# A hybrid decoder trunk on one core: the second weight slab's first quarter is brought and used ahead of the first slab, and one query copy and one partial mean change engines

## What is computed

```python
def even_mixer(xn, pos, lb, w_in, hgrn_gain, w_out):
    h = jnp.einsum('bsd,de->bse', xn, w_in)
    aq, af, ai, bq, bk, bv, z = jnp.split(h, splits, axis=-1)
    oa = hgrn2_chunked(heads(aq), heads(af), heads(ai), lb)   # gated recurrence
    ...
# in hgrn2_chunked:
    f = lbb + (1.0 - lbb) * jax.nn.sigmoid(to_chunks(f_logit))
    k = 1.0 - f
    b = jnp.cumsum(jnp.log(f), axis=3)
    q_dec = qc * jnp.exp(b)
    k_inv = k * jnp.exp(-b)
```

## Time and profile before

| | |
|---|---|
| times of three runs | 586.45, 587.00, 587.67 us (median 587.0) |
| the profiled execution | 587.2 us, its span 585.5 us |
| mean granted TensorE clock | 0.998 of full speed |
| PE busy | 575.8 us (98% of the span) |
| DVE, ACT, POOL busy | 416.2, 384.9, 73.3 us |
| read from HBM | 96.16 MB, 166 GB/s over the span |
| chain that ended last | PE 96%, ACT 1%, DVE 1%, DMA 1% |

### The profile page before, as it was taken

One profiled execution on the slowest core, in us unless ns is written; L12 is line 12 of the kernel. 1 busy time (PEld: TensorE's weight loads), 2 busy tenths in 40 slices (PEclk: granted clock), 3 DMA queues, 4 the chain that ended last, 5 costly groups with the idle time before them and its releaser, 6 DMA issues.

```text
span 585.5 us, 9718 instructions
## 1 busy us (share of the span) xinstructions
PE 575.8 (98%) x3868; PEld 532.9 (91%) x3868; DVE 416.2 (71%) x645; ACT 384.9 (66%) x583; POOL 73.3 (13%) x77
## 2 busy tenths in 40 slices
PE   7999999999999999999999999999999999999995
PEld 6999989999999898889988999999899998888985
DVE  6878579446977684567666874799997974766663
ACT  6854685278397575657666846969758837556764
POOL 4230005001003910100000001102120200100002
PEclk9999999999999999999999999999999999999999
DMA  9756364446624964465444544336644463356201
GB/s 297 251 180 222 89 201 143 146 143 217 208 81 150 282 217 144 153 232 190 144 144 163 198 151 177 128 123 213 218 144 145 161 234 128 128 213 219 104 1 73
DMA packets 51856, 98.88 MB, mean 169 GB/s; under 512 B 1732, under 2 KB 7140, under 8 KB 51812
## 3 DMA queue, kind: packets, MB, share of 16 engines
q1 hardware_dynamic: 50628, 96.95, 49.2%
q0 software_dynamic: 1024, 1.05, 0.7%
q10 hardware_dynamic: 160, 0.27, 0.1%
HBM read 96.16 MB, written 1.05 MB: 166 GB/s over the span
## 4 chain that ended last, share of the span: by engine, by line
PE 96%; ACT 1%; DVE 1%; DMA 1%; issue 0%; ACTq 0%; SPq 0%; DVEq 0%
PE proj L1773 17%; PE proj L1774 17%; PE proj L1775 17%; PE proj L1792 11%; PE proj L1793 11%; PE proj L1794 11%; PE head L2009 4%; PE head L2082 1%; PE head L2189 1%; PE head L1852 1%; DMA x_residual<-in_x_dram 1%; PE head L1986 1%; PE head L2054 1%; PE head L2220 1%; PE head L2091 1%; PE head L2017 0%
## 5 line engine op out<-in xcount | busy, mean ns | idle before, releaser
L1093 DVE TENSOR_TENSOR w_lo<-raw_weights,w_hi 128x1024 fp32r<-128x1024 f32 x174 | 224.4, 1305 | 104.4 <-ACT w_hi L515 102.7
L515 ACT ACTIVATE w_hi<-raw_weights 128x1024 fp32r<-128x1024 f32 x174 | 182.2, 1056 | 119.2 <-PE proj L1775 61.8
L1773 PE MATMUL proj<-xT_hi,w_hi 128*128 128x256 f32 x752 | 216.0, 287 | 0.1
L1775 PE MATMUL proj<-xT_hi,w_lo 128*128 128x256 f32 x752 | 212.8, 283 | 0.0
L1774 PE MATMUL proj<-xT_lo,w_hi 128*128 128x256 f32 x752 | 212.7, 283 | 0.0
L1773 PEld LDWEIGHTS proj<-xT_hi,w_hi 128*128 128x128 f32 x752 | 144.2, 192 | 1.1 <-issue 0.5
L1774 PEld LDWEIGHTS proj<-xT_lo,w_hi 128*128 128x128 f32 x752 | 144.2, 192 | 0.5
L1775 PEld LDWEIGHTS proj<-xT_hi,w_lo 128*128 128x128 f32 x752 | 144.2, 192 | 0.0
L1792 PE MATMUL proj<-w_hi,y_hi 128*128 128x512 f32 x176 | 69.4, 394 | 0.0
L1794 PE MATMUL proj<-w_lo,y_hi 128*128 128x512 f32 x176 | 68.5, 389 | 0.0
L1793 PE MATMUL proj<-w_hi,y_lo 128*128 128x512 f32 x176 | 68.5, 389 | 0.0
(11 more groups left out here) (296 smaller groups left out, 775.6 us busy)
## 6 DMA issues: line engine op xcount, KB each, us to landing
raw_weights<-in_ev_w_in_dram SPq DMA_DIRECT2D x15, 2048.0 KB, 8.4
raw_weights<-in_od_w_in_dram SPq DMA_DIRECT2D x12, 2048.0 KB, 8.6
raw_weights<-in_ev_w_out_dram SPq DMA_DIRECT2D x4, 2048.0 KB, 7.8
raw_weights<-in_xa_wkv_dram SPq DMA_DIRECT2D x4, 2048.0 KB, 8.3
raw_weights<-in_od_w_out_dram SPq DMA_DIRECT2D x4, 2048.0 KB, 7.7
raw_weights<-in_xa_wq_dram SPq DMA_DIRECT2D x2, 2048.0 KB, 9.0
raw_weights<-in_xa_wo_dram SPq DMA_DIRECT2D x2, 2048.0 KB, 8.4
x_residual<-in_x_dram SPq DMA_DIRECT2D x2, 512.0 KB, 3.9
```

The lines of the kernel that those rows point to most:

```text
L515: act.activation(ring_quarter(w_hi, n, q), raw_quarter(n, q), ACT.Copy).then_inc(hi_ready, 1)
L1093: dve.tensor_tensor(ring_quarter(w_lo, n, q), raw_quarter(n, q), ring_quarter(w_hi, n, q).bitcast(F32), ALU.subtract).then_inc(lo_ready, 1)
L1773: pe.matmul(dst, wh[:, k, :], x_hi[:, k, :], start=(k == 0), stop=False)
L1775: last = pe.matmul(dst, wl[:, k, :], x_hi[:, k, :], start=False, stop=(k == KC - 1))
```

## The change

SP brings quarter (1,0), rows 0 to 255 of slab 1 in runs of 2 KB, right behind `x`, then (0,0), (0,1) and the rest of slab 0 as before; slab 1's own transfer now leaves out its first two row blocks. The order in which quarters are made and used becomes (1,0), (0,0), (0,1), (0,2), (0,3), (1,1), ...; `place` and `quarter_at` translate between a quarter and its place, and from place 5 on nothing moves. The high part of (1,0) is split over ACT and DVE (first row block) and POOL (second row block); POOL makes the low parts of (1,0) and of (0,0). ACT makes the high part of (0,0) alone, between its fourth and fifth `xT_hi`. PE does all turns of `x` before any product, then (1,0), (0,0), (0,1), the turn of the 40 parameter rows (now into `head[1]`), (0,2), (0,3), (1,1) to (1,3). SP's wait before slab 2 asks for place 4, which is the low part of (0,3). The `ahead` calls of ACT and DVE stay where they were, and each now yields the quarter at the same place. In `last_cross` DVE copies the fourth query in place of ACT. In the last mean DVE adds two of the three parts, and ACT's square root takes its own third part and that sum.

```diff
+        def place(n, q):
+            return q + 1 if n == 0 else 0 if (n, q) == (1, 0) else 4 * n + q
+        def quarter_at(p):
+            return (1, 0) if p == 0 else (0, p - 1) if p < 5 else divmod(p, 4)
...
-            first_quarter(0)
-            first_quarter(1)
+            sp.dma_start(raw_quarter(1, 0), dram_slab(1)[:, 0:2, :]).then_inc(first_landed[0], 16)
+            for q in range(2):
+                sp.dma_start(raw_quarter(0, q), dram_slab(0)[:, :, P * q:P * q + P]).then_inc(first_landed[q + 1], 16)
...
-                    sp.wait_ge(lo_ready, 4 * (n - 1))
+                    sp.wait_ge(lo_ready, place(n - 2, 3) + 1)
+                if n == 2:
+                    sp.wait_ge(first_lo, 2)
...
+                k0 = 2 if n == 1 else 0
...
@@ gpsimd
-            pool.tensor_copy(ring_quarter(w_hi, 0, 0)[:, 6:8, :], raw_quarter(0, 0)[:, 6:8, :])
+            pool.tensor_copy(ring_quarter(w_hi, 1, 0)[:, 1, :], raw_quarter(1, 0)[:, 1, :])
             pool.drain().then_inc(first_hi_end, 1)
             pool.wait_ge(first_hi, 2)
+            pool.tensor_tensor(ring_quarter(w_lo, 1, 0), raw_quarter(1, 0), ring_quarter(w_hi, 1, 0).bitcast(F32),
+                               ALU.subtract).then_inc(first_lo, 1)
+            pool.wait_ge(hi_ready, 2)
             pool.tensor_tensor(ring_quarter(w_lo, 0, 0), raw_quarter(0, 0), ring_quarter(w_hi, 0, 0).bitcast(F32),
                                ALU.subtract).then_inc(first_lo, 1)
@@ scalar
-            act.activation(ring_quarter(w_hi, 0, 0)[:, 0:2, :], raw_quarter(0, 0)[:, 0:2, :], ACT.Copy).then_inc(first_hi, 1)
+            act.activation(ring_quarter(w_hi, 1, 0)[:, 0, 0:256], raw_quarter(1, 0)[:, 0, 0:256], ACT.Copy).then_inc(first_hi, 1)
             act.drain()
-            xT_high(0, 0, "ev_norm", 0)
+            xT_high(0, 0, "ev_norm", 0, range(4))
             act.wait_ge(first_landed[1], 16)
-            act.activation(ring_quarter(w_hi, 0, 1), raw_quarter(0, 1), ACT.Copy).then_inc(hi_ready, 2)
+            act.activation(ring_quarter(w_hi, 0, 0), raw_quarter(0, 0), ACT.Copy).then_inc(hi_ready, 2)
+            xT_high(0, 0, "ev_norm", 0, range(4, KC))
             ahead(-1, 3)
             ahead(slab("A", "f", 0), 0)
...
                 cross_high(1, 0)
-                query(nq, 3)
                 turned_probs(12 + 3, 2, 512)
...
-            act.drain()
-            act.activation(st[:, 5:6], st[:, 10:11], ACT.Identity, bias=st[:, 1:2])
-            act.wait_ge(last_part, 1)
-            root_of_tile(1, st[:, 3:4], st[:, 5:6])
+            act.wait_ge(early_ms, 2)
+            root_of_tile(1, st[:, 10:11], st[:, 5:6])
@@ vector
-            dve.tensor_copy(ring_quarter(w_hi, 0, 0)[:, 2:6, :], raw_quarter(0, 0)[:, 2:6, :]).then_inc(first_hi, 1)
+            dve.tensor_copy(ring_quarter(w_hi, 1, 0)[:, 0, 256:512], raw_quarter(1, 0)[:, 0, 256:512]).then_inc(first_hi, 1)
             dve.wait_ge(prm_ready, 1)
             xT_low(0, "ev_norm", 0)
-            dve.wait_ge(first_lo, 1)
-            dve.wait_ge(hi_ready, 2)
-            dve.tensor_tensor(ring_quarter(w_lo, 0, 1), raw_quarter(0, 1), ring_quarter(w_hi, 0, 1).bitcast(F32),
-                              ALU.subtract).then_inc(lo_ready, 2)
             ahead(-1, 3)
             ahead(slab("A", "f", 0), 0)
...
                 softmax_norm(24 + 6, 2, False)
+                dve.wait_ge(quarter_used, 4 * nq + 4)
+                dve.tensor_copy(blocks(0)[:, 3, :], bank(nq, 1, 1)[:, 0:S]).then_inc(last_query, 1)
+                dve.drain().then_inc(free_of(nq, 1, 1), 1)
                 cross_low(10, 0)
...
-            dve.drain().then_inc(last_part, 1)
+            dve.drain()
+            dve.wait_ge(last_sumsq, 3)
+            dve.tensor_scalar(st[:, 5:6], st[:, 3:4], st[:, 1:2], None, ALU.add).then_inc(early_ms, 1)
@@ tensor: turns of x, then
+            tile_turned(1, 3)
...
+            def first_slabs(f, i):
+                first_row_products(i)
+                first_column_products(f) 
+                slab_f(f, [1])
                 pe.wait_ge(early_prm_landed, 16 * 2)
-                pe.transpose(proj[2][:, 0:N_EARLY], prm_rows[0:N_EARLY, 0, :], ident[0:N_EARLY, 0:N_EARLY]
+                pe.transpose(head[1][:, 0:N_EARLY], prm_rows[0:N_EARLY, 0, :], ident[0:N_EARLY, 0:N_EARLY]
                              ).then_inc(prm_turned, 1)
-                slab_f(n, [2, 3])
+                slab_f(f, [2, 3])
                 pe.wait_ge(prm_ready, 2)
+                slab_t(i, [1, 2, 3])
```

More of the change, by code:

```diff
@@ L145, in hybrid_trunk @@
         head = [ctx.enter_context(nc.psum_tensor(f"head{i}", [P, 512], F32)) for i in range(4)]
-        first_landed = [sem(f"first_landed{q}") for q in range(3)]
+        first_landed = [sem(f"first_landed{q}") for q in range(4)]
         w_landed = [sem(f"w_landed{i}") for i in range(2)]
@@ L308, in filled @@
                 return
-            eng.wait_ge(quarter_used, 4 * n + (2 * u + 2 if kind == "F" else 2 * half + 2 if kind == "W" else 4))
+            eng.wait_ge(quarter_used, place(n, 2 * u + 1 if kind == "F" else 2 * half + 1 if kind == "W" else 3) + 1)
         def y_src(i):
@@ L503, in ahead @@
             def ahead(n, q):
[L505 removed]
+                p = 4 * n + q + 3
+                n, q = quarter_at(p)
                 if n >= NSLAB:
@@ L530, in root, with xT_high @@
                 act.activation(st[:, 6:8], st[:, 4:6], ACT.Sqrt).then_inc(rstd_ready, 1)
-            def xT_high(i, j0, gain, gk):
-                for k in range(KC):
+            def xT_high(i, j0, gain, gk, ks=range(KC)):
+                for k in ks:
                     if k < 4:
@@ L605, in _ @@
             act.wait_ge(prm_turned, 2)
-            act.activation(prm[:, KC:N_EARLY], proj[2][:, KC:N_EARLY], ACT.Copy).then_inc(prm_ready, 1)
+            act.activation(prm[:, KC:N_EARLY], head[1][:, KC:N_EARLY], ACT.Copy).then_inc(prm_ready, 1)
             act.wait_ge(lb_max, 1)
@@ L1885, in _, with first_row_products, first_column_products @@
             tile_turned(1, 2)
-            def first_quarter_products(n):
+            tile_turned(1, 3)
+            def first_row_products(n):
+                for t in range(T):
+                    take_bank(n, t)
+                wh, wl = ring_quarter(w_hi, n, 0), ring_quarter(w_lo, n, 0)
+                pe.wait_ge(prm_ready, 1)
+                pe.wait_ge(first_hi, 2)
+                for k in range(2):
+                    if k:
+                        pe.wait_ge(first_hi_end, 1)
+                    pe.wait_ge(xT_lo_ready, k + 1)
+                    for t in range(T):
+                        tok = slice(P * t, P * t + P)
+                        pe.matmul(bank(n, t)[:], xT_hi[:, k, tok], wh[:, k, :], start=(k == 0), stop=False)
+                        pe.matmul(bank(n, t)[:], xT_lo[:, k, tok], wh[:, k, :], start=False, stop=False)
+                pe.wait_ge(first_lo, 1)
+                for k in range(2):
+                    for t in range(T):
+                        last = pe.matmul(bank(n, t)[:], xT_hi[:, k, P * t:P * t + P], wl[:, k, :], start=False, stop=False)
+                last.then_inc(quarter_used, 1)
+            def first_column_products(n):
                 take_bank(n, 0)
-                pe.wait_ge(first_hi, 2)
+                pe.wait_ge(hi_ready, 2)
                 dst = bank(n, 0)[:, 0:S]
                 wh, wl = ring_quarter(w_hi, n, 0), ring_quarter(w_lo, n, 0)
[L1894 to L1898, removed]
                 for k in range(KC):
-                    if k == 6:
-                        pe.wait_ge(first_hi_end, 1)
                     pe.wait_ge(xT_lo_ready, k + 1)
@@ L1905, in first_quarter_products @@
                     pe.matmul(dst, wh[:, k, :], xT_lo[:, k, :], start=False, stop=False)
-                    if k == 0:
-                        tile_turned(1, 3)
-                    if 4 <= k < KC - 1:
-                        low([k - 4])
-                low(range(3, KC)).then_inc(quarter_used, 1)
-            def second_quarter_products(n):
-                pe.wait_ge(hi_ready, 2)
-                dst = bank(n, 0)[:, S:2 * S]
-                wh, wl = ring_quarter(w_hi, n, 1), ring_quarter(w_lo, n, 1)
-                for k in range(KC):
-                    pe.matmul(dst, wh[:, k, :], xT_hi[:, k, :], start=(k == 0), stop=False)
-                    pe.matmul(dst, wh[:, k, :], xT_lo[:, k, :], start=False, stop=False)
-                pe.wait_ge(lo_ready, 2)
+                pe.wait_ge(first_lo, 2)
                 for k in range(KC):
@@ L2077, in score @@
             def score(h, layer):
-                pe.wait_ge(q_rows, 4 + 4 * layer + h + 1)
+                if layer and h == 3:
+                    pe.wait_ge(last_query, 1)
+                else:
+                    pe.wait_ge(q_rows, 4 + 4 * layer + h + 1)
                 if h == 0:
```

40 lines of the change are left out of this document (17 added, 23 removed).

## The result

The changed kernel takes 589.69 us (median of six runs, 589.39 to 590.44), against 587.08 for the kernel before on the same chips: 1.0041 times as long, 95% interval 1.0028 to 1.0055. Measured a second time it took 589.94, ratio 1.0043 (1.0028 to 1.0058). So it is slower by 2.4 us by the ratio (2.6 by the medians), where 1.7 was forecast. The profiled execution took 589.47 us, 2.27 more than the one before, with a span of 587.4.

A forecast was written before the change was run, and what follows sets the result against it. PE, busy 575.8 of 585.5 us, was taken as the bound. Cast +0.1, parts 1 and 2 -0.4, part 3 +2.1 and part 4 -0.1 gave +1.7 on 587.0: 588.7 us, range 586.3 to 590.3.

The forecast's parts named there:

- the likeliest case: Slab 2 lands late and delays the ACT and DVE chain behind it: +1.7, 588.7 us, chance 0.55.
- the last rival: POOL and DVE block each other at the start, or slab 2 shares slab 3's queue: +2.8 to +3.5, 590.1, chance 0.15.
- Part 1: Start: PE dense from 9.88, parameter turn at 18.4; POOL's doubled cast costs 0.1; with Part 2, 0.4 gained.
- Part 2: Behind the parameter work: PE waits 1.1 to 1.2 for (0,3), going on at 22.6; with Part 1, 0.4 gained.
- Part 3: Slab 2, issued after (0,3)'s low part, lands at 31.0; the chain moves by 4.2 and PE loses 2.1.
- three waits forecast between 39 and 51: PE loses 0.2 at (2,2), 0.5 at (2,3) and 1.4 before the scores, waiting for `q_dec`.
- Part 4: The end: fourth query copied on DVE gains 0.1; the changed addition in the last mean counts 0.
- no wait stands behind the parameters: Rival: (0,3) is ready in time, so slab 2 also starts earlier; 585.4 us, chance 0.08.
- slab 2 is hidden: Rival: slab 2 lands by 29.2 or the scan's chain is shorter; only the start counts, 586.5, chance 0.22.
- the worse start: Rival: POOL and DVE block each other, or slab 2 shares slab 3's queue: +2.8 to +3.5, 590.1, chance 0.15.

The follow-up runs named there:

- the third experiment: The kernel before with one more wait on SP, so that slab 2 is issued late, nothing else; 589.99 us, ratio 1.0046.

## Why the prediction was right, and where a term was off

The mechanism of the likeliest case was the one that came, and slower by 2.4 us stands against +1.7 and inside the range of 586.3 to 590.3. By the number alone 589.69 lies nearer to the last rival (590.1) than to the forecast (588.7); the traces decide between them, not the time. In the start of the head outputs the sum of parts 1 to 3 was +1.8 (0.1 - 0.4 + 2.1); the traces have 2.16.

**Part 1** held. The T quarter and two F quarters ran dense, with the turn at 18.36 (18.4 forecast). The doubled cast on POOL took 0.86, and DVE's two halves of x beside it 1.23, where they took 1.11 before and 0.88 in the two traces in which the cast came behind them. That is 0.12 dearer, near the 0.1 of the forecast, but over the traces with the new start it is anywhere from 0.88 to 1.24. The first product started at 9.68, earlier by 0.2 where 0.1 later was forecast. It lies anywhere from 9.68 to 11.10 in the ten traces with the new start and from 9.63 to 9.94 in the four with the old one, with the landing of the first rows and weights; whether the new start has a part in the late ones is not shown.

**Part 2** named the mechanism, and its size was 0.7 short: PE got (0,3) at 23.29, not 22.6. The term that was mis-sized is the copied interval from the turn to the low part behind it: 2.88 in the row of the trace before, 21.91 - 18.36 = 3.55 in the changed kernel. 0.6 of the difference is POOL's fill, which held DVE's line 1208. The row was a lucky one: in the three other traces with the old order the interval is 3.25, 3.32 and 3.90. Front and first gap together gave +0.31 at the start of slab 2 (34.80 against 34.49), not -0.4.

**Part 3** is the heart, and the experiments show it from both sides. Slab 2 late, alone, makes the kernel before as slow as the change does (1.0046, of which 1.1 us is the slower landing with slab 3 close behind, and 1.0028 without that); slab 2 early takes all of the loss away (0.9981). Its terms: issue 22.6 forecast, 23.17 measured; landing 8.4, and 8.5; copy 31.05 and 31.69; scan 35.3 and 35.82; scores 50.7 and 51.06. So the chain from the copy to the scores was taken 0.3 too long (19.65, measured 19.37), which by luck hides part of the late issue. From 34.80 with five F quarters of 2.90 PE would have been at 49.3, so 1.8 were lost there in place of 2.1, because PE came 0.7 later and the scores 0.4 later. Of the three waits forecast between 39 and 51 this trace has two (0.33 and 1.02); the second trace of the same kernel has the third as well, 0.15 at 41.5. The forecast added the gap of part 2 and those of part 3; the table above shows that it is the sum that is fixed, by the chain behind slab 2, and that the first gap is free. The Trainium skill (DMA: Bandwidth & Descriptors, "Anatomy of one DMA") gives its fit, 6.8 us for this size, for transfers that GpSimd issues. The slabs are issued by SP, so the prediction had no ground to apply it here, and slab 2 took 8.5 to 9.7 in all traces. The full slabs of the changed kernel vary more than the prediction knew: the medians of their seven groups on the page run from 7.6 to 9.0.

**Part 4** was 0.1 and 0. The scores did come 0.1 earlier, and in these two traces the stretch from the head outputs to the end of the span is 0.26 shorter; but the time outside the span, 0.2 to 0.3 us longer by the medians than in the kernel before, was in no term of the sum, and takes that back. The changed mean moved nothing: the square root starts 0.97 after the end of the last addition before, and 0.99 after it in the changed kernel.

**The rivals.** That no wait stands behind the parameters is excluded by the 1.61 us gap. That slab 2 is hidden is excluded by the third experiment. Of the worse start, the sharing of the queue with slab 3 exists (1.1 us in the third experiment) but hardly reached the changed kernel, whose slab 3 came a microsecond later; the exclusion of DVE by POOL is real and sat at a third place, beside the parameter work. The Trainium skill's rule of an exclusive port pair (SBUF, State Buffer, "SBUF: two separate sides") agrees with the two rows on the fill; the rows on the doubled cast (1.23 in place of 1.11) do not settle it.

What stays open: why slab 2 took 9.1 with the fill moved and 8.5 to 8.8 in three executions with the same distance to slab 3; and why the time outside the span goes with the engine that copies the fourth query.

## What to carry to other kernels

When work is put in front of a pipeline that others fill by a fixed list of calls, count again how many units the consumer still has in hand at each place where the producers turn to other work; here one unit less turned a covered 4 us into a gap. Then look at what else waits for the same unit: the buffer that it frees, the transfer behind that, and the chain behind the transfer can cost more than the wait itself, and gaps in front of such a chain are free while the chain is late. One moved call that removes a wait at the start (the turns) gave most of what the whole rearrangement gives at its best.

## What the runs showed of the hardware that I had not expected

- Two slab transfers in flight on one queue slow the first: 2 MB landed in 9.6 and 9.7 us with the next issued 4.0 and 4.2 us behind, and in 8.5 and 8.6 in the same two kernels when the next waited for the landing. It is not constant otherwise: 8.5, 8.6, 8.8 and 9.1 in four traces with the next 5.1 or 5.2 behind, and 8.9 in one where the next was held back.
- A POOL fill of 128 x 1536 (1.38 us) held a DVE instruction on eight columns for its whole rest: 0.54 to 1.25 us in nine traces, ending 0.01 to 0.03 us behind the fill, and 0.16 or 0.17 in the five traces where the two did not meet.
- The granted clock fell to the 1.2 GHz level for some 3 us after PE gaps of 2.8 and 1.7 us near 33 to 36, and from 11 to 14 after gaps of 1.1 and 1.2 at the start of one execution; it stayed at full after gaps of 1.6 and 1.7 near 22, and after the same 1.1 and 1.2 at the start of another. The length of the gap alone does not tell.
- The time outside the span moved with one small edit near the end: in otherwise equal kernels it was 2.02 to 2.21 us with one small copy on DVE and 1.69 to 1.86 with it on ACT. The cause is not shown.
